# Rounding and subtracting the factors of seven-product block pairs two at a time

## The chip, the cores and the metric

The kernel runs on one core of one Trainium2 chip. The metric is the device time of one execution in microseconds (us). Lower is better. TensorE does the matmuls, VectorE (DVE in the rows) and ScalarE (ACT) work on whole 128-partition tiles, GpSimd is POOL, and SyncE (SP) issues most of the DMAs. PEld is TensorE's weight load, which runs beside its matmuls.

## The reference, cut to what matters

One layer of a decoder trunk for 512 prompt tokens and 8 sample tokens, 520 columns in all, model width 1024:

```python
z = rmsnorm(x, g1) @ w_in                         # q, k, v, o, gates, u, vb, ga, gb
y_a = (sigmoid(o) * mlstm(q, k, v, ...)) @ w_a
y_b = spatial_gate(gelu(u), rmsnorm(gelu(vb), g_v)) @ w_b
x = x + (sigmoid(ga) * y_a + sigmoid(gb) * y_b) @ w_o
up = rmsnorm(x, g2) @ w_up                        # width 2 * 2816
a, gval = split(causal_conv3(up) + c_b)
x = x + (silu(a) * gval) @ w_down
y = rmsnorm(x, g_final)
```

All of it is float32. The matmuls keep close to float32's precision by splitting each operand in two: a rounded part (hi, in the type fp32r) and the rest (lo = value - hi). A product is then hi·hi + hi·lo + lo·hi, three matmuls.

## The kernel before

**Tiling.** Data lie feature-major: 128 features on the partitions, 8 such blocks (`KT`), 520 tokens in two halves of 260 columns (`HALF`). A weight slot is 128 x 1024: eight 128 x 128 blocks side by side. Slots come in turn into two buffers `raw[0]` and `raw[1]` by SP's queue. ScalarE rounds a slot into `whi[t]` (`split`, L583, through the helper `A`, L580-581, so that every ScalarE row of the trace has L581), VectorE subtracts it into `wlo[t]` (`low`, L1079), and TensorE multiplies (`tile`, L1963; every matmul row has L1961). Two parities t alternate, so one slot is prepared while the other is multiplied.

**Block pairs.** In two places two output slots are computed together by a seven-product scheme in place of eight block products. Two neighbouring slots give a matrix of 2 x 2 blocks: a11 and a12 are the halves (512 columns, `HW`) of `raw[t0]`, a21 and a22 those of `raw[t1]`. The seven left factors are a11, a12, four sums of the blocks (`wsum`, or `dsum` in the down projection) and a22, in the order of `self.factor` (L288, L306). VectorE makes the four sums (`weight_sums` L1493, `down_weight_sums` L1705). Each factor f is rounded by ScalarE (`factor_hi`, L850, counted on the semaphore `s_ch`) and subtracted by VectorE (`factor_low`, L1488, counted on `s_pl`) into its place, half a buffer: factors 0 and 1 fill `whi[t0]` and `wlo[t0]`, factors 2 and 3 fill `whi[t1]` and `wlo[t1]`, factors 4 and 5 use t0 again and 6 uses t1. The right factors are quarters of the activations or combinations of them.

**Who waits for what.** TensorE multiplies a factor in `product` (L2175): it waits until `s_pl` has counted this factor, then issues 12 matmuls of 260 columns (4 blocks times 3 of hi and lo). The seven products of a pair follow each other, and full slots stand between pairs. ScalarE rounds factors 0 and 1 when the slot that last used t0 is done, and factors 2 and 3 when the slot that last used t1 is done (which is the last slot ahead of product 0) and the sums are there. In the down projection it waits for three of the four sums. VectorE's order in a pair is written out by hand: low of factors 0 and 1, the four sums, work on the last results, low of factors 2 and 3, and so on (`ay_pair` L1543, `down_pair` L1716).

**Where.** There are five gate pairs (q = 0 to 4, `gate_pair` L2195) and three down pairs (`down_pair` L2293 for TensorE). Product 0 of gate pair 0 begins near 354.7 us of the profiled span, those of gate pairs 1 to 4 near 376.5, 398.1, 419.6 and 441.2 us, and those of the down pairs near 782.3, 812.8 and 842.9 us. Between the first of a pair's slots and product 0 VectorE finishes the results of the pair ahead: `first_branch` (L1449, one operation) ahead of pairs 0 and 1, `branch_gated` (L1476, two operations) ahead of pairs 2 to 4. SP's queue reloads `raw[t0]` when the four sums are made (L533, L555) and `raw[t1]` when factor 6 is subtracted (L535, L559).

Of the kernel before, what the change touches and what calls it, by code (L numbers as in the profile page):

```python
# [17 lines left out]
F32 = mybir.dt.float32  # L18
F32R = mybir.dt.float32r
ALU = mybir.AluOpType  # L20
# [66 lines left out]
def hybrid_layer(nc, ins, outs):  # L87
    with ExitStack() as ctx:  # L88
# [59 lines left out]
        dsum = at("dsum", [P, 4, HW], F0 + 6688)  # L148
# [31 lines left out]
        wsum = at("wsum", [P, 4, HW], Q0 + 2 * XB)  # L180
# [5 lines left out]
        whi = [at(f"whi{t}", [P, KT * P], R0 + 8192 + (4096 + 32) * t, F32R) for t in range(2)]  # L186
        wlo = [at(f"wlo{t}", [P, KT * P], R0 + 16384 + 96 + (4096 + 64) * t, F32R) for t in range(2)]
# [87 lines left out]
        class Pair:  # L275


            def __init__(self, q):
                self.q = q
                self.n = [At(S_BY + 2 * WHOLE + 4 * q + t) for t in range(4)]  # L280
                self.of_b = q == 0
                self.t0, self.t1 = self.n[0].c % 2, self.n[1].c % 2
                self.j = WHOLE if self.of_b else 2 * q - 2
                self.a, self.d = (out_ps[self.t0][:, r, 0:HALF] for r in range(2))
                self.b, self.c = (out_ps[self.t1][:, r, 0:HALF] for r in range(2))
                r0, r1 = raw[self.t0], raw[self.t1]
                self.a11, self.a12, self.a21, self.a22 = r0[:, 0:HW], r0[:, HW:], r1[:, 0:HW], r1[:, HW:]
                self.factor = (self.a11, self.a12, wsum[:, 3, :], wsum[:, 1, :], wsum[:, 0, :], wsum[:, 2, :], self.a22)  # L288

            def place(self, w, f):  # L290

# [2 lines left out]
        class DownPair(Pair):  # L294


            def __init__(self, i):
                self.q = GATE_PAIRS + i
                self.i, self.j = i, 2 * i
                self.n = [At(S_DN + 6 * i + t) for t in range(8)]  # L300
                self.t0, self.t1 = self.n[4].c % 2, self.n[5].c % 2
                self.p1, self.p6 = (trp[t][:, :, :].rearrange("p a b -> p (a b)")[:, 0:HALF] for t in range(2))
                self.p5, self.p7 = (aux[:, t, 0:HALF] for t in range(2))
                r0, r1 = raw[self.t0], raw[self.t1]
                self.a11, self.a12, self.a21, self.a22 = r0[:, 0:HW], r0[:, HW:], r1[:, 0:HW], r1[:, HW:]
                self.factor = (self.a11, self.a12, dsum[:, 3, :], dsum[:, 1, :], dsum[:, 0, :], dsum[:, 2, :], self.a22)  # L306
                self.next_width = down_width(0 if i == DOWN_PAIRS - 1 else 1)

        def down_width(g):
# [269 lines left out]
        def _(act):  # L579
# [270 lines left out]
            def factor_hi(pr, f):  # L850

                A(pr.place(whi, f), pr.factor[f]).then_inc(s_ch, 1)

            def first_factors_hi(pr):

                act.wait_ge(w_loaded[pr.t0], pr.n[0].half(1) * 16)
                act.wait_ge(done, pr.n[0]())
                factor_hi(pr, 0)
                factor_hi(pr, 1)

            def next_factors_hi(pr):

                act.wait_ge(done, pr.n[1]())
                act.wait_ge(s_sw, 4 * pr.q + 4)
                factor_hi(pr, 2)
                factor_hi(pr, 3)

            def by_plain(i):
                n = At(S_BY + 2 * i)
# [119 lines left out]
            def down_pair(pr):  # L989
                q, n = pr.q, pr.n  # L990
                act.wait_ge(w_loaded[pr.t0], n[4].half(1) * 16)
                act.wait_ge(done, n[4]())
                factor_hi(pr, 0)
                factor_hi(pr, 1)
                act.wait_ge(s_sw, 4 * q + 3)
                act.wait_ge(done, n[5]())
                factor_hi(pr, 2)
                factor_hi(pr, 3)
                act.wait_ge(s_pd, 6 * q + 1)
                factor_hi(pr, 4)  # L1000
                A(dtmp[:, 1, :], pr.p1).then_inc(s_dc, 1)
                act.wait_ge(s_pd, 6 * q + 2)
                act.wait_ge(s_sw, 4 * q + 4)
                factor_hi(pr, 5)
                act.wait_ge(s_pd, 6 * q + 3)
                act.wait_ge(w_loaded[pr.t1], n[5].half(1) * 16)
                factor_hi(pr, 6)
                act.wait_ge(w_loaded[pr.t0], n[6].half(1) * 16)
                act.wait_ge(s_pd, 6 * q + 5)
                A(whi[pr.t0][:, 0:HW], raw[pr.t0][:, 0:HW]).then_inc(s_nh, 1)  # L1010
                act.wait_ge(s_pd, 6 * q + 6)
                A(whi[pr.t0][:, HW:pr.next_width], raw[pr.t0][:, HW:pr.next_width]).then_inc(w_hi, 3)
                split(n[7], down_width(1 if pr is pairs_d[-1] else 2))
# [62 lines left out]
        def _(dve):  # L1076
# [411 lines left out]
            def factor_low(pr, f):  # L1488

                dve.wait_ge(s_ch, 7 * pr.q + f + 1)  # L1490
                TT(pr.place(wlo, f), pr.factor[f], pr.place(whi, f).bitcast(F32), ALU.subtract).then_inc(s_pl, 1)  # L1491

            def weight_sums(pr):  # L1493

                for n in pr.n[0:2]:
                    dve.wait_ge(w_loaded[n.c % 2], n.half(1) * 16)
                TT(wsum[:, 0, :], pr.a21, pr.a22, ALU.add).then_inc(s_sw, 1)
                dve.drain()
                TT(wsum[:, 1, :], wsum[:, 0, :], pr.a11, ALU.subtract).then_inc(s_sw, 1)
                TT(wsum[:, 2, :], pr.a11, pr.a21, ALU.subtract).then_inc(s_sw, 1)  # L1500
                dve.drain()
                TT(wsum[:, 3, :], pr.a12, wsum[:, 1, :], ALU.subtract).then_inc(s_sw, 1)

            def first_gate_sum(pr):

# [4 lines left out]
            def by_plain(i):  # L1510
                n = At(S_BY + 1 + 2 * i)
                last = i == WHOLE - 1
                if i == NC:
                    unit_gated(NC * NH - 1)
                    low(n)
                    first_branch(n.plus(-2), i - 1, (i - 1) % 2)
                    x_difference(0, 1, 0)
                    unit_low(NC * NH - 1)
                    x_sum(2, KT // 2, 1)
                    dve.drain()  # L1520
                    x_difference(1, 2, 1)
                    x_difference(2, 2, 0)
                    low(n.plus(1))
                    x_combination_low(0, 1)
                    x_sum(3, KT // 2, 0)
                    dve.drain()
                    x_difference(3, 3, 2)
                    x_combination_low(2, 2)
                if last:
                    x_combination_low(1, 3)  # L1530
                    factor_low(pairs_w[0], 0)
                    factor_low(pairs_w[0], 1)
                    weight_sums(pairs_w[0])
                first_branch(n, i, i % 2)
                if last:
                    factor_low(pairs_w[0], 2)
                    factor_low(pairs_w[0], 3)
                    x_combination_low(3, 4)
                    first_gate_sum(pairs_w[0])
                else:  # L1540
                    low(n.plus(2))

            def ay_pair(pr):  # L1543
# [28 lines left out]
                if last:  # L1572
                    low(At(S_WO))
                    merged_low(pr.j)
                else:
                    factor_low(pairs_w[q + 1], 0)
                    factor_low(pairs_w[q + 1], 1)
                    weight_sums(pairs_w[q + 1])
                    if not pr.of_b:
                        merged_low(pr.j)  # L1580
# [4 lines left out]
                if last:  # L1585
                    low(At(S_WO + 1))
                else:
                    factor_low(pairs_w[q + 1], 2)
                    factor_low(pairs_w[q + 1], 3)
                    first_gate_sum(pairs_w[q + 1])  # L1590
                if not pr.of_b:
                    merged_low(pr.j + 1)
# [112 lines left out]
            def down_weight_sums(pr):  # L1705

                for n in pr.n[4:6]:
                    dve.wait_ge(w_loaded[n.c % 2], n.half(1) * 16)
                TT(dsum[:, 0, :], pr.a21, pr.a22, ALU.add).then_inc(s_sw, 1)
                dve.drain()  # L1710
                TT(dsum[:, 1, :], dsum[:, 0, :], pr.a11, ALU.subtract).then_inc(s_sw, 1)
                dve.drain()
                TT(dsum[:, 3, :], pr.a12, dsum[:, 1, :], ALU.subtract).then_inc(s_sw, 1)
                TT(dsum[:, 2, :], pr.a11, pr.a21, ALU.subtract).then_inc(s_sw, 1)

            def down_pair(pr):  # L1716
                q, n, j = pr.q, pr.n, pr.j
                part = lambda t, h: x1[:, j + t, h * HALF:(h + 1) * HALF]
                factor_low(pr, 0)
                factor_low(pr, 1)  # L1720
                down_weight_sums(pr)
                factor_low(pr, 2)
                factor_low(pr, 3)
                factor_low(pr, 4)
                factor_low(pr, 5)
                dve.wait_ge(s_pd, 6 * q + 3)
# [722 lines left out]
```

## Time and profile before

| | |
|---|---|
| median of 3 runs | 895.37 us (895.3 to 896.08) |
| the profiled execution | 896.04 us |
| its span, first to last instruction | 894.2 us |
| instructions | 18963 |
| matmuls | 7306 |
| mean TensorE clock granted | 0.996 of full speed |
| DMA | 100.44 MB, mean 112 GB/s |

How to read the rows: in a row of the timeline the columns are the start in the span, the duration (of all "x" instructions of the row, from the first's start to the last's end), the engine, the line, the operation, what it writes and reads, the shape, the count, and in brackets the idle time of the engine just before and what ended it. A duration covers the whole of an instruction, and the next one on the engine may start a little before it ends, so starts can be nearer to each other than durations. Matmuls overlap strongly: their rows last 0.28 us each, but they start 0.12 us apart.

### The profile page before, as it was taken

How to read it: one execution, taken by the hardware profiler on the slowest of the kernel's cores; microseconds unless marked ns; L12 is line 12 of the kernel's file. 1: busy time of each engine (PE TensorE's matmuls, PEld its weight loads, DVE VectorE, ACT ScalarE, POOL GpSimd, SP SyncE). 2: the span in 40 equal slices, each digit the busy share in tenths (PEclk: the TensorE clock that was granted, in tenths of full speed). 3: DMA queues.
4: the chain of work that ended last, by engine and by line, in shares of the span. 5: the costliest groups of instructions: out<-in, count | busy, mean ns of one | idle time of the engine just before them, and what ended most of it. 6: DMA issues, size and time to landing. Idle time of an engine off the chain costs nothing.

```text
span 894.2 us, 18963 instructions
## 1 busy us (share of the span) xinstructions
PE 886.6 (99%) x7306; PEld 881.9 (99%) x7306; DVE 609.9 (68%) x980; ACT 390.5 (44%) x629; POOL 133.0 (15%) x182
## 2 busy tenths in 40 slices
PE   9999999999999999999999999999999999999997
PEld 9999999999999999999999999999999999999997
DVE  7886775443885568677755777777777778966543
ACT  7545434544873334344432344444444444432333
POOL 0673000002542110000005800000000000000001
PEclk9999999999999999999999999999999999999998
DMA  6332252234872222322255222222222222333232
GB/s 214 107 131 89 77 196 101 84 100 149 291 269 69 67 76 75 116 95 95 96 197 135 89 81 94 94 94 94 94 93 86 83 91 87 99 107 93 85 106 96
DMA packets 31499, 100.44 MB, mean 112 GB/s; under 512 B 4668, under 2 KB 7260, under 8 KB 31192
## 3 DMA queue, kind: packets, MB, share of 16 engines
q1 hardware_dynamic: 29256, 92.96, 31.1%
q0 software_dynamic: 1472, 5.72, 2.1%
q10 hardware_dynamic: 720, 1.04, 0.4%
q8 instruction: 36, 0.59, 0.3%
q14 instruction: 15, 0.12, 0.0%
HBM read 92.37 MB, written 7.35 MB: 112 GB/s over the span
## 4 chain that ended last, share of the span: by engine, by line
PE 91%; POOLq 3%; issue 3%; DMA 1%; POOL 1%; ACT 0%; SPq 0%; ACTq 0%
PE out L1961 84%; PE trp L1961 3%; PE aux L1961 2%; POOLq L1939 2%; POOLq L1937 1%; PE trp L1995 1%; DMA cwb<-in_conv_wb 1%; DMA raw_pair<-in_w_slots 1%; PE aux L2153 0%; POOL y L1952 0%; POOL out_conv_old L1923 0%; ACT xg L581 0%; POOL sct L1927 0%; POOLq L1930 0%; POOLq L88 0%
## 5 line engine op out<-in xcount | busy, mean ns | idle before, releaser
L581 ACT ACTIVATE whi<-raw_pair 128x1024 fp32r<-128x1024 f32 (+4 forms) x168 | 154.2, 924 | 207.4 <-PE out L1961 195.6
L1083 DVE TENSOR_TENSOR wlo<-raw_pair,whi 128x1024 fp32r<-128x1024 f32 (+1 forms) x121 | 155.2, 1282 | 86.8 <-ACT whi L581 86.4
L1961 PE MATMUL out<-xh,whi 128*128 128x260 f32 x668 | 143.5, 289 | 0.0
L1961 PE MATMUL out<-x2h,whi 128*128 128x260 f32 x704 | 141.8, 283 | 0.0
L1961 PE MATMUL out<-x2l,whi 128*128 128x260 f32 x704 | 141.3, 282 | 0.0
L1961 PE MATMUL out<-x2h,wlo 128*128 128x260 f32 x704 | 141.2, 282 | 0.0
L1961 PE MATMUL out<-xl,whi 128*128 128x260 f32 x668 | 139.0, 282 | 0.0
L1961 PE MATMUL out<-xh,wlo 128*128 128x260 f32 x668 | 139.0, 282 | 0.0
L1961 PEld LDWEIGHTS out<-x2h,whi 128*128 128x128 f32 x704 | 108.4, 188 | 0.1
L1961 PEld LDWEIGHTS out<-x2h,wlo 128*128 128x128 f32 x704 | 108.3, 188 | 0.0
L1961 PEld LDWEIGHTS out<-x2l,whi 128*128 128x128 f32 x704 | 108.3, 188 | 0.0
L1961 PEld LDWEIGHTS out<-xh,whi 128*128 128x128 f32 x668 | 105.2, 188 | 0.7 <-issue 0.2
L1961 PEld LDWEIGHTS out<-xl,whi 128*128 128x128 f32 x668 | 104.9, 188 | 0.0
L1961 PEld LDWEIGHTS out<-xh,wlo 128*128 128x128 f32 x668 | 104.9, 188 | 0.0
L1961 PE MATMUL out<-acth,whi 128*128 128x260 f32 (+2 forms) x266 | 58.2, 284 | 0.0
L1961 PE MATMUL out<-actl,whi 128*128 128x260 f32 (+2 forms) x266 | 57.8, 282 | 0.0
L1961 PE MATMUL out<-acth,wlo 128*128 128x260 f32 (+2 forms) x266 | 57.8, 282 | 0.0
L1645 DVE TENSOR_TENSOR up<-out,rbc 128x520 f32<-128x520 f32 x44 | 30.8, 700 | 37.5 <-PE out L1961 37.3
L1945 POOL COPY nconv<-up 128x10 f32 x44 | 10.4, 237 | 240.1 <-DVEq L1646 240.1
L581 ACT ACTIVATE acth<-silu 128x520 f32 (+1 forms) x22 | 14.1, 639 | 69.8 <-DVE silu L1660 69.8
L1961 PEld LDWEIGHTS out<-acth,whi 128*128 128x128 f32 x266 | 42.9, 188 | 0.2 <-DVE wlo L1491 0.2
L1961 PEld LDWEIGHTS out<-actl,whi 128*128 128x128 f32 x266 | 42.8, 188 | 0.0
(362 smaller groups left out, 1758.0 us busy)
## 6 DMA issues: line engine op xcount, KB each, us to landing
raw_pair<-in_w_slots SPq DMA_DIRECT2D x123, 512.0 KB, 3.3
raw_pair<-in_w_dn SPq DMA_DIRECT2D x16, 448.0 KB, 3.3
c_ring<-in_C_state SPq DMA_DIRECT2D x8, 512.0 KB, 5.1
row<-scratch SPq DMA_DIRECT2D x8, 512.0 KB, 5.9
out_C_sample<-c_ring SPq DMA_DIRECT2D x8, 512.0 KB, 4.3
raw_pair<-in_w_dn SPq DMA_DIRECT2D x8, 512.0 KB, 3.5
xres<-in_x_all POOLq DMA_DIRECT2D x1, 1560.0 KB, 6.8
x<-in_x_all SPq DMA_DIRECT2D x5, 260.0 KB, 6.7
```

The lines of the kernel that those rows point to most:

```text
L581: return act.activation(out, in_, func, **kw_)
L1083: TT(wlo[p][:, 0:width], raw[p][:, 0:width], whi[p][:, 0:width].bitcast(F32), ALU.subtract)\
L1645: TT(both(up[t][:, 2:2 + TOK]), out2(n), both(rbc2[:, :]), ALU.mult).then_inc(evac[n.c % 2], 1)
L1937: pool.drain()
L1939: pool.drain()
L1945: pool.tensor_copy(nconv[:, i * 2 + t, :], up[t][:, SEQ:2 + TOK]).then_inc(s_nc, 1)
L1961: return pe.matmul(*a, **k)
L1995: m = pe.transpose(trp[b.c % 2][:, c, :], ftmp[b.c % 2][:, c * P:(c + 1) * P], ident[:, :])
```

## The change

Factors 0 and 1 lie side by side in `raw[t0]`, and their places lie side by side in `whi[t0]` and `wlo[t0]`. The four sums are put in another order in `wsum` and `dsum`, so that factors 2 and 3 lie side by side as well. Then one operation of 1024 columns rounds factors 0 and 1, another factors 2 and 3, and the same holds for the subtraction. Each raises its semaphore by 2 when it ends. The subtraction waits until both factors are rounded. TensorE's code, the order of the steps on each engine, the factors 4 to 6 and the DMAs are not edited.

```diff
@@ class Pair (and the same in DownPair, with dsum)
-                self.factor = (self.a11, self.a12, wsum[:, 3, :], wsum[:, 1, :], wsum[:, 0, :], wsum[:, 2, :], self.a22)
+                self.factor = (self.a11, self.a12, wsum[:, 0, :], wsum[:, 1, :], wsum[:, 2, :], wsum[:, 3, :], self.a22)
+                self.two = (r0, wsum[:, 0:2, :].rearrange("p a b -> p (a b)"))
@@ ScalarE
+            def two_factors_hi(pr, h):
+
+                A(whi[pr.t1 if h else pr.t0][:, :], pr.two[h]).then_inc(s_ch, 2)
+
             def first_factors_hi(pr):
...
                 act.wait_ge(done, pr.n[0]())
-                factor_hi(pr, 0)
-                factor_hi(pr, 1)
+                two_factors_hi(pr, 0)
 
             def next_factors_hi(pr):
 
                 act.wait_ge(done, pr.n[1]())
                 act.wait_ge(s_sw, 4 * pr.q + 4)
-                factor_hi(pr, 2)
-                factor_hi(pr, 3)
+                two_factors_hi(pr, 1)
@@ ScalarE, down_pair
-                factor_hi(pr, 0)
-                factor_hi(pr, 1)
+                two_factors_hi(pr, 0)
                 act.wait_ge(s_sw, 4 * q + 3)
                 act.wait_ge(done, n[5]())
-                factor_hi(pr, 2)
-                factor_hi(pr, 3)
+                two_factors_hi(pr, 1)
@@ VectorE
+            def two_factors_low(pr, h):
+
+                t = pr.t1 if h else pr.t0
+                dve.wait_ge(s_ch, 7 * pr.q + 2 * h + 2)
+                TT(wlo[t][:, :], pr.two[h], whi[t][:, :].bitcast(F32), ALU.subtract).then_inc(s_pl, 2)
+
             def weight_sums(pr):
...
-                TT(wsum[:, 0, :], pr.a21, pr.a22, ALU.add).then_inc(s_sw, 1)
-                dve.drain()
-                TT(wsum[:, 1, :], wsum[:, 0, :], pr.a11, ALU.subtract).then_inc(s_sw, 1)
-                TT(wsum[:, 2, :], pr.a11, pr.a21, ALU.subtract).then_inc(s_sw, 1)
-                dve.drain()
-                TT(wsum[:, 3, :], pr.a12, wsum[:, 1, :], ALU.subtract).then_inc(s_sw, 1)
+                TT(wsum[:, 2, :], pr.a21, pr.a22, ALU.add).then_inc(s_sw, 1)
+                dve.drain()
+                TT(wsum[:, 1, :], wsum[:, 2, :], pr.a11, ALU.subtract).then_inc(s_sw, 1)
+                TT(wsum[:, 3, :], pr.a11, pr.a21, ALU.subtract).then_inc(s_sw, 1)
+                dve.drain()
+                TT(wsum[:, 0, :], pr.a12, wsum[:, 1, :], ALU.subtract).then_inc(s_sw, 1)
```

In `down_weight_sums` the places change in the same way and the order in time stays. In the five places of VectorE's program where `factor_low(pr, 0)` and `factor_low(pr, 1)`, or 2 and 3, were called one after the other, `two_factors_low(pr, 0)` or `two_factors_low(pr, 1)` is called (in `by_plain`, `ay_pair` and `down_pair`).

## Rows read from the trace of the kernel before

**Rows 1.** The page, part 1: busy time, share of the span, instructions, by engine

```profile
PE 886.6 (99%) x7306; PEld 881.9 (99%) x7306; DVE 609.9 (68%) x980; ACT 390.5 (44%) x629; POOL 133.0 (15%) x182
```

**Rows 2.** Windows: length, busy by engine (count), granted clock, DMA share, GB/s

```profile
core 0: us, PE busy (x) PEld busy (x) DVE busy (x) ACT busy (x) POOL busy (x), PEclk, DMA share, GB/s
4.00:6.30 2.30, 1.83 (x9) 1.54 (x8) 0.83 (x2) 0.93 (x3) 0.00 (x0) 1.00 0.90 267
340.00:376.00 36.00, 36.00 (x299) 35.66 (x298) 28.43 (x40) 13.45 (x21) 0.00 (x0) 1.00 0.26 89
884.00:894.00 10.00, 4.44 (x30) 3.99 (x28) 3.18 (x10) 1.42 (x4) 1.93 (x3) 0.68 0.63 213
```

**Rows 3.** Waits of the weight load: waiter, releaser, us in total, times, longest

```profile
PEld out L1961 <- issue: 0.9, 2, 0.8
PEld out L1961 <- DVE wlo L1491: 0.2, 1, 0.2
```

**Rows 4.** Groups of instructions by form: shapes, count, busy us, mean ns, idle before

```profile
L1083 DVE TENSOR_TENSOR wlo<-raw_pair,whi 128x1024 fp32r<-128x1024 f32 x108 | 141.0, 1305 | 69.9 <-ACT whi L581 69.6
L1491 DVE TENSOR_TENSOR wlo<-wsum,whi 128x512 fp32r<-128x512 f32 x20 | 12.9, 685 | 0.2 <-ACT whi L581 0.2
L581 ACT ACTIVATE whi<-raw_pair 128x1024 fp32r<-128x1024 f32 x108 | 114.4, 1059 | 121.9 <-PE out L1961 120.8
L581 ACT ACTIVATE whi<-wsum 128x512 fp32r<-128x512 f32 x20 | 11.6, 623 | 20.2 <-PE out L1961 15.6 <-DVE wsum L1502 4.6
```

**Rows 5.** Timelines of ScalarE, VectorE and the weight load at gate pair 0

```profile
356.25 1.15 ACT L581 ACTIVATE whi<-wsum 128x512 fp32r<-128x512 f32 x2 [4.63 <-DVE wsum L1502]
...
356.91 1.29 DVE L1491 TENSOR_TENSOR wlo<-wsum,whi 128x512 fp32r<-128x512 f32 x2 [0.15 <-ACT whi L581]
...
357.36 0.19 PEld L1961 LDWEIGHTS out<-xh,wlo 128*128 128x128 f32 x1
357.72 0.19 PEld L1961 LDWEIGHTS out<-xh,whi 128*128 128x128 f32 x1 [0.17 <-issue]
```

**Rows 6.** The same timelines at gate pair 1

```profile
376.70 1.15 ACT L581 ACTIVATE whi<-wsum 128x512 fp32r<-128x512 f32 x2 [4.53 <-PE out L1961]
...
377.36 1.29 DVE L1491 TENSOR_TENSOR wlo<-wsum,whi 128x512 fp32r<-128x512 f32 x2
...
379.27 0.19 PEld L1961 LDWEIGHTS out<-xh,whi 128*128 128x128 f32 x1
```

**Rows 7.** The same timelines at gate pair 2, and VectorE's ahead of it

```profile
393.98 1.29 DVE L1491 TENSOR_TENSOR wlo<-raw_pair,whi 128x512 fp32r<-128x512 f32 x2
395.19 0.69 DVE L1497 TENSOR_TENSOR wsum<-raw_pair 128x512 f32<-128x512 f32 x1
...
398.25 1.16 ACT L581 ACTIVATE whi<-wsum 128x512 fp32r<-128x512 f32 x2 [3.51 <-PE out L1961]
...
399.36 0.70 DVE L1481 TENSOR_TENSOR merged<-merged,ftmp 128x520 f32<-128x520 f32 x1
399.97 0.69 DVE L1491 TENSOR_TENSOR wlo<-wsum,whi 128x512 fp32r<-128x512 f32 x1
...
400.83 0.19 PEld L1961 LDWEIGHTS out<-xh,whi 128*128 128x128 f32 x1
```

**Rows 8.** VectorE's timeline after gate pair 4: a subtraction 1024 wide

```profile
458.64 1.22 DVE L1083 TENSOR_TENSOR wlo<-raw_pair,whi 128x1024 fp32r<-128x1024 f32 x1
459.78 0.70 DVE L1486 TENSOR_TENSOR ml<-merged,mh 128x520 fp32r<-128x520 f32 x1
```

**Rows 9.** Timelines of VectorE, ScalarE and the weight load at down pair 0

```profile
780.53 1.22 DVE L1491 TENSOR_TENSOR wlo<-raw_pair,whi 128x512 fp32r<-128x512 f32 x2
...
783.96 1.67 ACT L581 ACTIVATE whi<-dsum 128x512 fp32r<-128x512 f32 x3 [5.21 <-DVE dsum L1713]
...
784.62 0.69 DVE L1491 TENSOR_TENSOR wlo<-dsum,whi 128x512 fp32r<-128x512 f32 x1
...
782.22 0.19 PEld L1961 LDWEIGHTS trp<-acth,whi 128*128 128x128 f32 x1
...
785.37 0.19 PEld L1961 LDWEIGHTS out<-acth,whi 128*128 128x128 f32 x1 [0.19 <-DVE wlo L1491]
```

**Rows 10.** Timelines of ScalarE and the weight load at down pair 1

```profile
813.03 1.15 ACT L581 ACTIVATE whi<-dsum 128x512 fp32r<-128x512 f32 x2 [3.86 <-PE out L1961]
...
815.43 0.19 PEld L1961 LDWEIGHTS out<-acth,wlo 128*128 128x128 f32 x1
815.55 0.19 PEld L1961 LDWEIGHTS out<-acth,whi 128*128 128x128 f32 x1
```

More of the change, by code:

```diff
@@ L305, in __init__ @@
                 self.a11, self.a12, self.a21, self.a22 = r0[:, 0:HW], r0[:, HW:], r1[:, 0:HW], r1[:, HW:]
-                self.factor = (self.a11, self.a12, dsum[:, 3, :], dsum[:, 1, :], dsum[:, 0, :], dsum[:, 2, :], self.a22)
+                self.factor = (self.a11, self.a12, dsum[:, 0, :], dsum[:, 1, :], dsum[:, 2, :], dsum[:, 3, :], self.a22)
+                self.two = (r0, dsum[:, 0:2, :].rearrange("p a b -> p (a b)"))
                 self.next_width = down_width(0 if i == DOWN_PAIRS - 1 else 1)
@@ L1530, in by_plain @@
                     x_combination_low(1, 3)
-                    factor_low(pairs_w[0], 0)
-                    factor_low(pairs_w[0], 1)
+                    two_factors_low(pairs_w[0], 0)
                     weight_sums(pairs_w[0])
@@ L1535, in by_plain @@
                 if last:
-                    factor_low(pairs_w[0], 2)
-                    factor_low(pairs_w[0], 3)
+                    two_factors_low(pairs_w[0], 1)
                     x_combination_low(3, 4)
@@ L1575, in ay_pair @@
                 else:
-                    factor_low(pairs_w[q + 1], 0)
-                    factor_low(pairs_w[q + 1], 1)
+                    two_factors_low(pairs_w[q + 1], 0)
                     weight_sums(pairs_w[q + 1])
@@ L1587, in ay_pair @@
                 else:
-                    factor_low(pairs_w[q + 1], 2)
-                    factor_low(pairs_w[q + 1], 3)
+                    two_factors_low(pairs_w[q + 1], 1)
                     first_gate_sum(pairs_w[q + 1])
@@ L1708, in down_weight_sums @@
                     dve.wait_ge(w_loaded[n.c % 2], n.half(1) * 16)
-                TT(dsum[:, 0, :], pr.a21, pr.a22, ALU.add).then_inc(s_sw, 1)
+                TT(dsum[:, 2, :], pr.a21, pr.a22, ALU.add).then_inc(s_sw, 1)
                 dve.drain()
-                TT(dsum[:, 1, :], dsum[:, 0, :], pr.a11, ALU.subtract).then_inc(s_sw, 1)
+                TT(dsum[:, 1, :], dsum[:, 2, :], pr.a11, ALU.subtract).then_inc(s_sw, 1)
                 dve.drain()
-                TT(dsum[:, 3, :], pr.a12, dsum[:, 1, :], ALU.subtract).then_inc(s_sw, 1)
-                TT(dsum[:, 2, :], pr.a11, pr.a21, ALU.subtract).then_inc(s_sw, 1)
+                TT(dsum[:, 0, :], pr.a12, dsum[:, 1, :], ALU.subtract).then_inc(s_sw, 1)
+                TT(dsum[:, 3, :], pr.a11, pr.a21, ALU.subtract).then_inc(s_sw, 1)
             def down_pair(pr):
@@ L1718, in down_pair @@
                 part = lambda t, h: x1[:, j + t, h * HALF:(h + 1) * HALF]
-                factor_low(pr, 0)
-                factor_low(pr, 1)
+                two_factors_low(pr, 0)
                 down_weight_sums(pr)
-                factor_low(pr, 2)
-                factor_low(pr, 3)
+                two_factors_low(pr, 1)
                 factor_low(pr, 4)
```

## The prediction

> **What bounds the kernel now.** I began with the page's busy shares: TensorE is busy for 99% of the span, VectorE for 68%, ScalarE for 44% [rows 1]. The windows show the same in the stretch of the first gate pair: 36.00 of 36.00 us, at the full granted clock of 2.4 GHz [rows 2]. So the end moves only with TensorE's own work, which is not edited, or with a wait put in front of it. The waits of its weight load (the first part of the engine that sees a missing factor) are small: one of 0.2 us is for the subtraction of factors, and another 0.17 us in gate pair 0 is put down to "issue" but lies at the same join [rows 3, 5]. What decides is therefore not how much work VectorE and ScalarE have in all, but how late each factor is, and I read the timelines at each join next, then the groups by form for the durations.
>
> **The durations.** A 512-wide rounding takes 0.62 us, one of 1024 takes 1.06; a 512-wide subtraction 0.685 [rows 4]. For a 1024-wide subtraction the group's mean is 1.305 us over the whole kernel [rows 4], but 1.22 in the stretch of the pairs, where the next one starts 1.14 us after it [rows 8]; two 512-wide ones take 1.21 from start to next start [rows 7]. So each fusion saves VectorE 0.07 us. For ScalarE two overlapped roundings last 1.15 us against 1.06, 0.09 saved [rows 4, 5]. Against that the first factor of the two comes later: rounding 1.06 - 0.62 = 0.44, subtraction 1.22 - 0.68 = 0.54, together 0.98 us. TensorE needs the first factor first, so this is the time at stake. Product 0 or 2 now waits for the pair; product 1 or 3 for no more than before, less some hundredths.
>
> **Factors 0 and 1.** They are prepared one slot ahead. At gate pair 2 their subtractions start at 393.98, while factors 2 and 3 of the same pair, after the four sums, are wanted only at 400.83 [rows 7], and product 0's own weights two products of 12 x 0.12 = 1.44 us earlier, about 397.95. The narrowest place is down pair 0: both subtractions there end at 780.53 + 1.22 = 781.75 and product 0 loads at 782.22 [rows 9], so even a factor 0 that comes with factor 1 is 0.47 us early. Cost 0 at all eight pairs; with a delay at the group's mean duration still 0. The sums start up to 0.37 us later where the subtraction waits for the wider rounding (pairs 1 and down pairs 1 and 2), in idle time of VectorE. In down pair 0 it does not wait, since the rounding ends long before 780.53, and the sums there, which release ScalarE at 783.96, stay where they are or come 0.07 earlier.
>
> **Factors 2 and 3, gate pair 0.** ScalarE is released by the last sum at 356.25. Before: the first rounding ends at 356.87, the subtraction begins at 356.91 and ends at 357.59, and the weights are loaded at 357.72, where the steady step of 0.12 from 357.36 would have given 357.48 [rows 5]: a stall of 0.24 already. After: rounding to 357.31, subtraction from 357.35 to 358.57, load at 358.70. Added: 0.98 us.
>
> **Gate pair 1.** ScalarE starts at 376.70, so rounding ends at 377.76; VectorE is free at 377.36, and subtracts from 377.80 to 379.02. With 0.06 (down pair 0, 785.31 to 785.37) to 0.13 us (gate pair 0) from the subtraction's end to the load this is 379.08 to 379.15, and product 2 wants 379.27 [rows 5, 6, 9]. Added: 0, with 0.1 us left of cover.
>
> **Gate pairs 2 to 4.** Here two operations for the results of the pair ahead stand before the subtraction in VectorE's queue, so it starts at 399.97 though the rounding (398.25 + 1.06 = 399.31) has ended. The 0.07 saved earlier in this queue brings it to 399.90. It ends at 401.12 and the load follows at 401.18 to 401.25, against 400.83 [rows 7]. Before, the end at 400.66 met it just in time. Added: 0.35 to 0.42, I take 0.39, and the same in pairs 3 and 4, where the distance from ScalarE's release to the subtraction is again 1.72 us: 1.17 us in three pairs. If VectorE is a little earlier than I think it stays some 0.3 each; at a duration of 1.305 it is 0.47.
>
> **Down pair 0.** VectorE works without a break here and the sum releases ScalarE at 783.96. Before: the first subtraction begins at 784.62, ends at 785.31, and the load comes at 785.37 after 0.19 us idle [rows 9]. After: 0.98 later, 786.35. Added: 0.98, or 0.91 if the 0.07 saved ahead reaches the sums.
>
> **Down pairs 1 and 2.** Release at 813.03, rounding to 814.09, subtraction from 814.13 to 815.35, load at 815.41 to 815.48; wanted at 815.55 [rows 10]. Added: 0, with about 0.1 us left; at worst 0.1 each.
>
> What else waits: factor 4's rounding is queued behind the wide one on ScalarE, which ends 0.09 earlier than the two; its subtraction likewise comes earlier. The reload of `raw[t0]` follows the sums and has several us until it is used; that of `raw[t1]` follows factor 6. Nothing else in the change has a cost. The increments of 2 are new for these semaphores only in size, and I price them at 0, between -0.1 and +0.1 at each of the two unhidden joins.
>
> **The sum.** 0.98 + 0 + 1.17 + 0.98 + 0 = 3.13 us. A delay of TensorE goes to the end in full: behind the gates it is busy throughout, and its later releasers are themselves started by its results. The profiled execution took 896.04 us, 1.84 more than its span of 894.2; with the change it would be 899.2. It lies at the upper edge of the three runs (895.3 to 896.08), so from the median 895.37 the forecast is 898.5 us.
>
> The page "VectorE: DVE Perf Modes" of the Trainium skill, section "The TRN2 errata — SBUF-src ops pay a fixed extra latency per instruction", says that the fixed cost lies between instructions, so that one large tile pays it once, and it advises wide tiles; by its formula for a float32 tensor_tensor, (N + 151) / 0.96 ns, I estimate 1.224 us for 1024 columns. The trace agrees with 1.22. That rule speaks for the change and knows nothing of who waits for the first half; what it would bring alone is the second rival.
>
> **The rivals.**
> *Only two joins show.* If VectorE's queue ahead of gate pairs 2 to 4 is earlier by 0.4 us after the change than my 0.07 (the merged results wait for TensorE and ScalarE too, and may close up), pairs 2 to 4 stay hidden: + 1.96, so 897.3 us. For it: the cover before was just enough in three pairs, with no idle time of the load there. Against it: VectorE runs from 393.98 on without a gap down to the subtraction, and only 0.07 is taken out of that.
>
> *The saved fixed costs reach the end; not slower.* The mechanism: VectorE, not TensorE, paces the pairs, above all the unbroken stretch ahead of down pair 0, so 16 fused subtractions at 0.07 give 1.1 us: 894.3 us. It decides from the point at which rounding and subtraction of both factors end no later than the first factor did, 1.31 us after the release; the rows make it 2.28. Against it also: TensorE's waits for VectorE at these joins are under 0.5 us in all, so no more than that can be had unless TensorE waits longer than the rows show. By the skill's page alone, fewer instructions are always a gain, and this is its case.
>
> *The clock falls.* The gaps ahead of product 2 grow from 0.24 to 1.2 us in two places. In the last 10 us of the span, where TensorE is busy for 4.44, the granted clock averages 0.68, so part of it is at the lower level of 1.2 GHz; but between 4.00 and 6.30, with 0.47 us idle, it is 1.00 [rows 2]. Each of the seven products takes 1.44 us; if three of them after each of the two gaps ran at half clock, 2 x 3 x 1.44 = 8.6 us are added to 3.1: 907 us. The page "TensorE: Matmul & The Clock Gate", Part 1, has the same two levels and idleness as what brings the lower one; no row here shows a fall after a gap as short as 1.2 us.
>
> *It does not do what it says*: the semaphore would be raised before the whole width is written, or TensorE would not feel the wait: 895.4 us.
>
> **How the numbers follow.** A measurement of this kernel can tell 0.2%, 1.8 us, from no change. Forecast (two large and three small stalls, 897.9 to 899.3): 0.68. Only two joins: 0.16. Saved costs reach the end: 0.06. The clock: 0.04. No effect: 0.06. The slower side of the bound is at 897.2: the forecast gives 0.66 of its 0.68, the first rival 0.11 of 0.16 (its 897.3 is at the edge), the clock 0.04, together 0.81. Same: 0.02 + 0.05 + 0.06 from no effect + 0.02 of the saved costs = 0.15. Faster: 0.04. The range reaches down to 896.9, which takes in most of the first rival and medians that are off by some tenths, and up to 900.0, with 0.47 in each of gate pairs 2 to 4, 0.1 in gate pair 1 and the two down pairs, and some tenths of the runs' own spread; the clock, the saved costs and no effect are left out.
>
> **What would show it.** The weight load should have five waits for the fused subtraction: at gate pair 0 and down pair 0 about 1.1 to 1.2 us, at gate pairs 2 to 4 about 0.3 us (0.39 less the 0.07 by which durations overlap the step), and none at gate pair 1 and down pairs 1 and 2. The 1024-wide subtractions should take 1.22 us, and the matmul count and clock should not change. I am wrong if pair 2's product 2 loads on the 0.12 us step, if the stalls are there and the span has not grown by their sum (then something later gave it back), or if product 0 waits anywhere.

## The result and the profile after

Over eight runs each, the changed kernel takes 898.72 us (898.28 to 899.44) and the kernel before 895.66 us (895.08 to 896.8). The ratio is 1.0033, with a 95% interval of 1.0023 to 1.0043: slower by about 3 us (2.1 to 3.9). The profiled execution takes 898.83 us with a span of 897.0. All ratios, here and below, are of fast runs alone: one slow execution of eleven in split_two_big (4973.73 us) and one of twelve in early (2245.13 us) are not in them.

The page of the changed kernel says what the totals did: its length and its busy shares.

```profile
span 897.0 us, 18947 instructions
...
PE 885.9 (99%) x7306; PEld 880.8 (98%) x7306; DVE 609.3 (68%) x964; ACT 388.9 (43%) x613; POOL 133.2 (15%) x182
```

Against [rows 1] VectorE and ScalarE have 16 instructions fewer each, VectorE 0.6 us and ScalarE 1.6 us less to do, TensorE the same 7306 matmuls; and the span is 2.8 us longer. The waits of the weight load in the changed kernel (to be read against [rows 3]; L1499 is the wide subtraction):

```profile
PEld out L1963 <- issue: 3.5, 5, 1.3
PEld out L1963 <- DVE wlo L1499: 1.2, 1, 1.2
```

The waits of its matmuls name the wide subtraction at all five places:

```profile
PE out L1963 <- DVE wlo L1499: 2.6, 5, 1.1
```

The kernel before had two waits on "issue"; now there are five. One of them (1.14 us at 6.4 us in the span) belongs to the start of the kernel. The other four are the joins of factor 2 at gate pairs 0 and 2 to 4; the wait of 1.2 us is down pair 0. The weight load's timeline has these four loads, each the first of a product 2, and between the first two of them the load of product 2 at gate pair 1 (380.35) with the one ahead of it, which keeps its step of 0.12 us:

```profile
358.80 0.19 PEld L1963 LDWEIGHTS out<-xh,whi 128*128 128x128 f32 x1 [1.30 <-issue]
...
380.23 0.19 PEld L1963 LDWEIGHTS out<-xh,wlo 128*128 128x128 f32 x1
380.35 0.19 PEld L1963 LDWEIGHTS out<-xh,whi 128*128 128x128 f32 x1
...
402.31 0.19 PEld L1963 LDWEIGHTS out<-xh,whi 128*128 128x128 f32 x1 [0.34 <-issue]
...
424.27 0.19 PEld L1963 LDWEIGHTS out<-xh,whi 128*128 128x128 f32 x1 [0.34 <-issue]
...
446.22 0.19 PEld L1963 LDWEIGHTS out<-xh,whi 128*128 128x128 f32 x1 [0.34 <-issue]
```

A load lasts 0.19 us and the next starts 0.12 us after it starts, so an idle time of 0.34 is a delay of 0.34 + 0.07 = 0.41 us. Below, "delay" is always this: the distance between two starts less 0.12. A single one is good to about 0.01 us.

The chain at gate pair 0 after the change, ScalarE then VectorE, to be read against [rows 5]; then at gate pair 2, against [rows 7]; then at down pair 0 with its load, against [rows 9]:

```profile
356.30 1.06 ACT L583 ACTIVATE whi<-wsum 128x1024 fp32r<-128x1024 f32 x1 [4.81 <-DVE wsum L1510]
357.46 1.23 DVE L1499 TENSOR_TENSOR wlo<-wsum,whi 128x1024 fp32r<-128x1024 f32 x1 [0.68 <-ACT whi L583]
...
399.38 1.06 ACT L583 ACTIVATE whi<-wsum 128x1024 fp32r<-128x1024 f32 x1 [3.56 <-PE out L1963]
400.98 1.22 DVE L1499 TENSOR_TENSOR wlo<-wsum,whi 128x1024 fp32r<-128x1024 f32 x1
...
786.23 1.58 ACT L583 ACTIVATE whi<-dsum 128x1024 fp32r<-128x1024 f32 x2 [5.27 <-DVE dsum L1717]
787.39 1.22 DVE L1499 TENSOR_TENSOR wlo<-dsum,whi 128x1024 fp32r<-128x1024 f32 x1 [0.64 <-ACT whi L583]
788.67 0.19 PEld L1963 LDWEIGHTS out<-acth,whi 128*128 128x128 f32 x1 [1.20 <-DVE wlo L1499]
```

At gate pair 0 ScalarE starts at 356.30, nearly as before (356.25), but the first weights that TensorE can use are complete at 357.46 + 1.23 = 358.69 instead of 357.59.

The accounts: delays of 1.37 (gate pair 0), 3 x 0.41 (gate pairs 2 to 4) and 1.27 (down pair 0) make 3.87 us, against 0.24 and 0.26, 0.50 in all, before: 3.37 us more. The last group of sums at the end starts 3.28 us later (889.69 against 886.41), so the stalls arrive there in full, to a tenth. The span is only 2.8 longer because of the tail, which the last section explains.

### The profile page after: what moved, and what is told of

It is laid out like the page before. It is cut to its first block, busy times and chain, and to the rows that moved or that the text cites. A ratio compares the mean times of both kernels' runs of the same rounds, so it can differ in the third digit from the quotient of the medians.

```text
span 897.0 us, 18947 instructions
## 1 busy us (share of the span) xinstructions
PE 885.9 (99%) x7306; PEld 880.8 (98%) x7306; DVE 609.3 (68%) x964; ACT 388.9 (43%) x613; POOL 133.2 (15%) x182
## 3 DMA queue, kind: packets, MB, share of 16 engines
q10 hardware_dynamic: 720, 1.04, 0.4%
## 4 chain that ended last, share of the span: by engine, by line
PE 83%; DVE 5%; issue 4%; POOLq 3%; DMA 2%; DVEq 2%; POOL 1%; ACT 1%; SPq 0%; ACTq 0%
PE out L1963 76%; PE trp L1963 3%; PE aux L1963 2%; POOLq L1941 2%; POOLq L1939 1%; DMA raw_pair<-in_w_slots 1%; PE trp L1997 1%; DMA cwb<-in_conv_wb 1%; DVE wlo L1499 1%; DVE wlo L1085 1%; DVEq L1506 0%; DVE dtl L1707 0%; ACT whi L583 0%; PE aux L2155 0%; DVE wsum L1510 0%
```

## The experiments

The theory: product 2 waits for the first half of its factors, which comes about 1 us later as half of a wide operation; all the loss is there. The rivals were: a share from factors 0 and 1 or from the new places of the sums; the fixed costs saved reaching the end; for the smaller stalls, another cause than VectorE's queue.

The median of before moves between the series of runs (895.6 to 895.9 us), so the ratio is what is compared. The delays are those of one profiled execution each, and a sum of them is good to some hundredths.

| kernel | delay, gate pair 0 | gate pairs 2 to 4, each | down pair 0 | all | median | ratio to before |
|---|---|---|---|---|---|---|
| before | 0.24 | 0 | 0.26 | 0.50 | 895.66 | |
| changed | 1.37 | 0.41 | 1.27 | 3.87 | 898.72 | 1.0033 (1.0023 to 1.0043) |
| only01 | 0.71 | 0 | 0.18 | 0.89 | 895.68 | 0.9999 (0.999 to 1.0008) |
| only23 | 1.74 | 0.48 | 1.34 | 4.52 | 899.18 | 1.0037 (1.0024 to 1.0051) |
| split_two_big | 0.16 | 0.41 | 0.19 | 1.57 | 896.65 | 1.0008 (0.9998 to 1.0017) |
| hidden_only | 0.14 | 0 | 0.19 | 0.33 | 895.48 | 0.9995 (0.9986 to 1.0004) |
| round_only | 0.38 | 0 | 0.66 | 1.04 | 896.25 | 1.0012 (1.0003 to 1.002) |
| subtract_only | 1.13 | 0.40 to 0.46 | 1.31 | 3.71 | 898.84 | 1.0035 (1.0022 to 1.0048) |
| between | 1.07 | 0.51 (product 4) | 1.27 | 3.87 | 899.17 | 1.0044 (1.0031 to 1.0057) |
| early | 0 | 0.51 (product 4) | 0 | 1.53 | 896.71 | 1.0009 (1.0 to 1.0018) |
| between_later | 1.01 | 0 | 1.27 | 2.28 | 897.64 | 1.0021 (1.0012 to 1.003) |
| best_split | 0 | 0 | 0 | 0 | 895.28 | 0.9992 (0.9983 to 1.0001) |
| best_wide | 0 | 0 | 0 | 0 | 894.96 | 0.9992 (0.9983 to 1.0001) |

**Which pair of factors.** Both helpers choose by `h` (0: factors 0 and 1; 1: factors 2 and 3):

```diff
+                if h == 0:          # only01; h == 1 in only23
                     A(whi[pr.t1 if h else pr.t0][:, :], pr.two[h]).then_inc(s_ch, 2)
+                else:
+                    factor_hi(pr, 2 * h)
+                    factor_hi(pr, 2 * h + 1)
... (the same for the subtraction)
```

> Only factors 0 and 1 are rounded and subtracted as one; 2 and 3 go one by one, with the sums in the new places. Theory (the first of factors 2 and 3 comes 0.98 us later, and product 2 waits): no stall of product 0 anywhere, the stalls of the kernel before stay at 0.17 and 0.19 us of load idle, time as before, 895.7 us, within 0.3. Rival A (part of the loss comes from the fusion of 0 and 1, through later sums or a later reload): 0.5 to 1.5 us over before, and idle of the weight load at product 0 or later sums at pairs 1 to 4. Rival B (the new places of the sums cost): every join a little later, over 896.5 us.

> Only factors 2 and 3 are rounded and subtracted as one, in all eight pairs. Theory: all of the loss is here: 3.1 us over before, 898.8 us, with load idle of 1.3 us at gate pair 0, 1.2 at down pair 0 and, since 0.07 us of VectorE's queue is no longer saved ahead of them, 0.41 in place of 0.34 at gate pairs 2 to 4 (so up to 0.2 more than the changed kernel). Rival A: 0.5 to 1.5 us less than the changed kernel.

Only01 measures as before (0.9999), with no stall at a product 0; its sums have the new places too, so the places cost nothing that can be told. Only23 has all of the loss: 1.0037. One expectation was wrong: in only01 the delay at gate pair 0 was 0.71 us and not 0.24, though the pair there is split. These are its first sum, its rounding and its load:

```profile
353.81 0.69 DVE L1513 TENSOR_TENSOR wsum<-raw_pair 128x512 f32<-128x512 f32 x1 [2.36 <-DMA raw_pair<-in_w_slots]
...
356.77 1.15 ACT L583 ACTIVATE whi<-wsum 128x512 fp32r<-128x512 f32 x2 [5.19 <-DVE wsum L1518]
...
358.25 0.19 PEld L1971 LDWEIGHTS out<-xh,whi 128*128 128x128 f32 x1 [0.65 <-issue]
```

The sums wait for a transfer. Counted from the load that opens the slot ahead (348.88 in before, 348.92 here), the first sum starts at 4.41 us in before and at 4.89 here, and between 4.13 and 4.89 over these profiles; it moves with the transfer and not with the edit (4.89 also in only23, where factors 0 and 1 are split). From ScalarE's start to the load the distance is then the same in all runs of a kind: 1.47 or 1.48 us where both are split (before 357.72 - 356.25, only01 358.25 - 356.77), 2.50 or 2.51 where both are fused (changed, only23, between). So the fusion's own price from ScalarE's start on is 1.03 us at gate pair 0, and the later sums add 0.1 us in the changed kernel's profile. At down pair 0 the same distance is 1.41 where both are split (785.37 - 783.96) and 2.44 where both are fused (788.67 - 786.23): again 1.03.

**The two places and the hidden ones.** The condition is `not (h == 1 and pr.q in (0, 5))` in split_two_big and `h == 0 or pr.q in (1, 6, 7)` in hidden_only (down pairs have q = 5 to 7).

> The changed kernel, but factors 2 and 3 of gate pair 0 and of down pair 0 go one by one. Theory: the two large stalls go back to 0.17 and 0.19 us of load idle, the three of 0.34 at gate pairs 2 to 4 stay: 1.2 us over before, 896.9 us, 1.9 under the changed kernel. Rival (the delays are given back later, or one stall hides another): less than 1.2 us under the changed kernel, and new idle of the load behind the two places.

> Factors 0 and 1 fused in all pairs, factors 2 and 3 only in gate pair 1 and down pairs 1 and 2, where some tenth of a us of cover was left. Theory: as before, 895.7 us within 0.3, with 11 operations fewer on each of VectorE and ScalarE and no new load idle: an operation saved there is worth nothing. Rival (the saved fixed costs reach the end): 0.07 us for each fused subtraction, 0.8 us under before, 894.9 us.

Both came as the theory has them: removing two stalls left the other three at 0.41. In hidden_only 11 fused operations on each engine move no time that can be told (0.9995, interval over 1), and the delays alone, 0.33 against 0.50, would give 0.9998. That fits no gain beyond the stalls, but the interval doesn't exclude the rival's 0.8 us.

**The two halves of the price.** In round_only the rounding is always fused and the subtraction for `h == 0` alone; subtract_only is the reverse.

> The changed kernel, but factors 2 and 3 are subtracted one by one; their rounding stays one operation. Theory: the first factor loses only the 0.44 us of the wider rounding, and only where VectorE waits for ScalarE: +0.45 to 0.5 at gate pair 0 and at down pair 0 (load idle about 0.65 each), 0 at gate pairs 2 to 4, where the rounding ends 0.6 us before VectorE is free. 0.9 us over before, 896.6 us. Rival (stall is the subtraction's alone): as before, 895.7. Rival (any wide operation costs the same): 1.5 us over before.

> The changed kernel, but factors 2 and 3 are rounded one by one; their subtraction stays one operation, so it waits for the second rounding. Theory: the two roundings take 1.15 us against 1.06, so the first factor comes 0.09 us later than in the changed kernel at gate pair 0 and down pair 0, and no later at gate pairs 2 to 4: 3.25 us over before, 898.9 us; gate pair 1 and down pairs 1 and 2 keep about 0 of cover and may show up to 0.1 each. Rival (the loss is shared between the two operations by their widths): about half of the changed kernel's loss, 897.2.

Down pair 0 in round_only, ScalarE, VectorE and the load:

```profile
783.92 1.58 ACT L583 ACTIVATE whi<-dsum 128x1024 fp32r<-128x1024 f32 x2 [5.26 <-DVE dsum L1725]
...
785.02 2.50 DVE L1497 TENSOR_TENSOR wlo<-dsum,whi 128x512 fp32r<-128x512 f32 x4 [0.58 <-ACT whi L583]
...
785.76 0.19 PEld L1971 LDWEIGHTS out<-acth,whi 128*128 128x128 f32 x1 [0.59 <-DVE wlo L1497]
```

The rounding alone costs 0.48 us there (0.66 against the 0.18 of only01), and at gate pair 0 the distance from ScalarE's start is 1.90 against 1.47. The delay there is only 0.38 us, less than expected, because this profile has the earliest sums (4.13 us after the load that opens the slot ahead). Gate pairs 2 to 4 do not feel the wider rounding. With the subtraction fused and the rounding split the distance is 2.59, the 0.09 us more of two roundings; at gate pair 1 and down pairs 1 and 2, where up to 0.1 us was expected, subtract_only has 0.02 each. The ratio of round_only, 1.0012, is 0.5 us more than its delays say; its interval holds them.

**VectorE's queue.** In between, the wide subtraction stands ahead of the second operation for the last results:

```diff
                 TT(both(ftmp[g][:, :]), both(ftmp[g][:, :]), out2(n), ALU.mult).then_inc(evac[n.c % 2], 1)
+                if ahead is not None:     # two_factors_low(pairs_w[q + 1], 1)
+                    ahead()
                 dve.drain()
                 TT(merged[:, j, :], merged[:, j, :], ftmp[g][:, :], ALU.add).then_inc(s_ms, 1)
```

> The changed kernel with one step moved in VectorE's queue ahead of gate pairs 2 to 4: the wide subtraction stands between the two operations for the last results (after the one that empties the accumulator, ahead of the addition into merged). Theory: it starts when the rounding ends, 0.5 us earlier, so the load of product 2 comes on the step again at gate pairs 2 to 4: 1.2 us under the changed kernel, 897.5 us, with the idle of 1.3 and 1.2 us unchanged. Rival (the stalls there are TensorE's handoff and not VectorE's queue): as the changed kernel, 898.7. Rival (the later addition delays the merged results): new idle of the load at the first output-projection slots, over 898 us.

The time did not fall: 899.17 us, where 897.5 was expected. The stall at product 2 was gone, as the theory has it, but a new one of 0.51 us stood at product 4. ScalarE, VectorE and the load:

```profile
402.30 0.64 ACT L583 ACTIVATE mh<-merged 128x520 fp32r<-128x520 f32 x1 [2.15 <-DVE merged L1489]
402.84 0.37 ACT L583 ACTIVATE gtmp<-out 128x260 f32<-128x260 f32 x1
...
403.24 0.42 DVE L1526 TENSOR_TENSOR ftmp<-gtmp,out 128x260 f32<-128x260 f32 x1 [0.98 <-ACT gtmp L583]
...
405.00 0.19 PEld L1974 LDWEIGHTS out<-th,whi 128*128 128x128 f32 x1 [0.44 <-issue]
```

The addition into `merged` came later, ScalarE stood at the rounding of these results for 2.15 us, and behind it in its queue stood the copy of product 0 (`gtmp`), for which VectorE waited 0.98 us ahead of factor 4's subtraction. The third rival had the later addition and the time right, and the place wrong: the stall is inside the pair and not at the output projection. In between_later these two steps stand behind factor 4 of the next pair:

```diff
                 A(gtmp[:, 0, :], pr.a).then_inc(s_pc, 1)
                 factor_hi(pr, 4)
+                if q >= 2:
+                    merged_hi(pairs_w[q - 1].j + 1)
... (the same for merged_low behind factor_low(pr, 4) on VectorE; the old calls stay for the last pair alone)
```

> As the run in which the wide subtraction stands between VectorE's two operations for the last results, and in addition the rounding and the subtraction of these results (merged_hi and merged_low of the pair's second slot) stand behind factor 4 of the next pair, on both engines. Theory (in the run before the stall moved from product 2 to product 4, because the late addition held back ScalarE's copy of product 0, which stands behind merged_hi in its queue): no load idle at gate pairs 2 to 4 at all, delays only at gate pair 0 (0.9 to 1.7 us, by when the transfer for the sums lands) and down pair 0 (1.27): 1.2 to 1.5 us under the changed kernel, 897.4 us. Rival (product 4 is late for the wide subtraction itself, which takes VectorE too long): the 0.44 us of load idle at product 4 stay, 898.7.

No delay is left at gate pairs 2 to 4, and the ratio falls from 1.0044 to 1.0021. So the stalls of the changed kernel there were VectorE's queue, and the one of between came from the work on the last results standing ahead of factor 4.

**Versions meant to beat both.** Early adds two edits to between and splits factors 2 and 3 in gate pair 0 and down pair 0; best_wide adds the same to between_later, and best_split to hidden_only:

```diff
                 TT(wsum[:, 1, :], wsum[:, 2, :], pr.a11, ALU.subtract).then_inc(s_sw, 1)
-                TT(wsum[:, 3, :], pr.a11, pr.a21, ALU.subtract).then_inc(s_sw, 1)
                 dve.drain()
                 TT(wsum[:, 0, :], pr.a12, wsum[:, 1, :], ALU.subtract).then_inc(s_sw, 1)
+                TT(wsum[:, 3, :], pr.a11, pr.a21, ALU.subtract).then_inc(s_sw, 1)
...
-                act.wait_ge(s_sw, 4 * pr.q + 4)
+                act.wait_ge(s_sw, 4 * pr.q + 3)
... (ahead of factor_hi(pr, 5))
+                act.wait_ge(s_sw, 4 * q + 4)
...
-            dve.memset(acc[:, :], 0.0).then_inc(s_accf, 1)
             down_pair(pairs_d[0])
+            dve.memset(acc[:, :], 0.0).then_inc(s_accf, 1)
```

> The version that should beat both: factors 2 and 3 fused except in gate pair 0 and down pair 0; the wide subtraction between the two operations as in the run before; in the gate pairs the sum for factor 2 is made third and ScalarE waits for three sums; the clearing of the norm accumulator, 0.49 us on VectorE ahead of down pair 0, comes after that pair. Theory: no stall at any of the eight pairs, also not the 0.24 us and 0.26 us of the kernel before: 0.5 us under before, 895.2 us, near what the runs can tell; the trace has the verdict. Rival (the old stalls have another cause than VectorE's late sums): the load idle of 0.17 and 0.19 us stays, and 895.7 us.

> Factors 2 and 3 fused only in gate pair 1 and down pairs 1 and 2, nothing moved in the work on the last results; the sum for factor 2 made third in the gate pairs with ScalarE waiting for three sums, and the clearing of the norm accumulator put behind down pair 0. Theory: no load idle at any pair: 0.5 us of local delay fewer than before, 895.2 us, with the run's own uncertainty as large. Rival (the earlier rounding does not help, since VectorE does the subtraction at the same time): 0.17 and 0.19 us of load idle stay, 895.7.

> As the run above, but factors 2 and 3 fused in gate pairs 2 to 4 too, with the order of the first run of this call there. Theory: no load idle at any pair either, and the same time, 895.2 us: fewer operations on VectorE and ScalarE are worth nothing while TensorE waits for none. Rival (saved operations are a gain in themselves): under the run above by 0.2 us or more.

Early missed its 895.2 us: it measured 896.71, because it carries the stall of between, 0.51 us in each of three pairs. In the two others there is none: these are all waits of the weight load in best_wide from 340 to 870 us, and neither is at a block pair.

```profile
PEld aux L1979 <- POOLq L1957: 0.3, 1, 0.3
PEld out L1979 <- DVE wlo L1092: 0.2, 1, 0.2
```

Both kernels have a ratio of 0.9992, with an interval that just holds 1: the 0.5 us that the trace shows gone (0.9994) fits, and is not shown by the times. The wide form and the split form cannot be told apart: their ratios are the same, and their medians differ by 0.32 us (894.96 against 895.28), less than the half microsecond that the tail alone can make (last section). So the rival of best_wide, that saved operations are worth 0.2 us or more, is not excluded.

**The wait in front of an operation that raises its semaphore by 2.** Two handoffs from ScalarE to VectorE in the changed kernel, first of a full slot, then of factors 2 and 3 at gate pair 1; both roundings and both subtractions are 1024 wide:

```profile
366.37 1.06 ACT L583 ACTIVATE whi<-raw_pair 128x1024 fp32r<-128x1024 f32 x1 [0.80 <-PE out L1963]
367.46 1.22 DVE L1085 TENSOR_TENSOR wlo<-raw_pair,whi 128x1024 fp32r<-128x1024 f32 x1 [0.72 <-ACT whi L583]
...
377.83 1.06 ACT L583 ACTIVATE whi<-wsum 128x1024 fp32r<-128x1024 f32 x1 [4.65 <-PE out L1963]
378.99 1.23 DVE L1499 TENSOR_TENSOR wlo<-wsum,whi 128x1024 fp32r<-128x1024 f32 x1 [0.52 <-ACT whi L583]
```

The full slot's subtraction, which raises its semaphore by 1, starts 0.03 us after the rounding ends (367.43), the other 0.10 us (378.89). The trace shows the difference: a subtraction that raises by 1 holds its wait in itself, while none of the 48 operations of ScalarE and VectorE in the changed kernel that raise by 2 or 3 does; their wait is an instruction of its own. This is L1498, `wait_ge` in `two_factors_low` (duration in ns: shortest, median, longest; the kernel before has no such instruction for `factor_low`):

```profile
L1498 DVEq EVENT_SEMAPHORE  x16: 21/21/21, 350.1 to 847.6; - x16
```

That it goes with the operation's own raise, and not with the width or with the rounding's raise, three other rows say: a subtraction 384 wide that raises by 3 (L1740 of the kernel before, 821.68 + 0.53 to 822.31) also starts 0.10 us after its rounding; in subtract_only, where the roundings raise by 1, the wide subtraction still starts 0.10 us after them; in round_only a 512-wide one, which raises by 1, starts 0.04 us after a wide rounding that raises by 2 (784.98 to 785.02). ScalarE has the same thing: at down pair 0 its wide rounding starts 0.09 us after the sum ends (785.45 + 0.69 to 786.23), the 512-wide one in the kernel before 0.04 (783.23 + 0.69 to 783.96). There too it is not the width: full-slot roundings, 1024 wide, start 0.02 us after TensorE has counted its slot as done, the fused ones of gate pairs 1 to 4 start 0.07 us after it. No run kept the wide operations and raised by 1. As an estimate from these rows, that would give back 0.12 us at down pair 0 and 0.07 at gate pair 0, of the 1.0 and 1.1 us that are lost there.

## Why the prediction was right

*The sum* was 3.13 us and the ratio gives 2.96 us (0.0033 x 895.66), medians 3.06. 898.5 was forecast and 898.72 measured. The interval of the ratio is 0.9 us to either side, so the times alone cannot weigh the terms, and that the sum is met to 0.2 us is in part luck. The delays of the traces can: they add up to 3.37, 0.24 more than forecast, and the terms below share it.

*Gate pair 0, forecast 0.98.* The profile has 1.13 more. The wider rounding (0.43) and the wider subtraction (0.53) came as worked out. Mis-sized was the raise by 2, which was priced at 0, between -0.1 and +0.1: the subtraction starts 0.07 us later for it (357.36 to 357.46, where 0.04 was taken), which makes the 1.03. The last 0.1 us are the sums, which a transfer released 0.09 us later in this profile. ScalarE's release there was treated as fixed, which it is not.

*Gate pairs 2 to 4, forecast 0.39 each.* 0.41 each, for the reason given: the subtraction waits for VectorE's queue and not for ScalarE, so the wider rounding costs nothing. The wide subtraction starts 0.92 us ahead of the step on which the load is wanted (400.98 against 402.31 - 0.41 = 401.90), the narrow one 0.86 us ahead (399.97 against 400.83): 0.06 earlier, where 0.07 was forecast.

*Gate pair 1 and down pairs 1 and 2, forecast 0.* They load on the step, as shown for gate pair 1. The cover was thinner than the forecast 0.1 us, since the raise by 2 counts here too, on both engines: the subtraction starts at 378.99 and ends at 380.22, and the load comes at 380.35, 0.13 us later, where gate pair 0 needs 0.11 (358.69 to 358.80). It held by about 0.02.

*Down pair 0, forecast 0.98, or 0.91 with the 0.07 saved ahead.* 1.01 more: 1.03 from ScalarE's start to the load, 0.05 by which ScalarE starts later after the sum, less 0.08 that the fusion of factors 0 and 1 gives back (0.26 to 0.18 in only01). The parts were named, and the raise by 2 was again the term that was too small, by 0.12 on the two engines together.

*Factors 0 and 1, forecast 0.* Only01 shows it: no delay at a product 0, and a ratio of 0.9999.

*The rivals.* Only two joins: refuted, the other three stalls are in every profile that has the wide subtraction at that place of the queue (changed, only23, split_two_big, subtract_only). The saved fixed costs: refuted in sign for the change as a whole; the wide operation that pays its fixed cost once is the one that comes late. That a part of the saved cost reaches the end where no stall stands against it is not excluded (hidden_only, best_wide). That it does nothing: refuted. The clock: refuted, by the windows of the gate pairs and from down pair 0 on in the changed kernel (length, busy time of each engine, granted clock, DMA share, GB/s), where the clock is 1.00 through gaps of up to 1.3 us:

```profile
340.00:466.00 126.00, 124.40 (x1032) 123.51 (x1031) 89.72 (x132) 48.88 (x74) 1.10 (x3) 1.00 0.30 101
786.00:870.00 84.00, 83.01 (x693) 82.80 (x693) 48.73 (x75) 27.04 (x38) 0.00 (x0) 1.00 0.34 99
```

*The signs.* Five waits of the load came, where they were said to be, of 1.30 and 1.20 us (1.1 to 1.2 forecast) and three of 0.34 (about 0.3); no product 0 waits. One sign of being wrong did show: the span grew by 2.8 us and not by the 3.37 of the delays. Something later gave some 0.5 us back, the clock of the last matmuls (last section), on which the forecast had no word.

## What to carry to other kernels

Where a consumer takes two halves in turn, fuse the two producing steps only if the first half has at least as much slack as the wide operation lasts longer than the narrow one, on every engine that the consumer's chain waits for (here 0.43 + 0.53 us), plus what a raise by 2 costs in front of each (here 0.05 and 0.07 us). Read that slack at each join by itself: for factors 2 and 3 it was enough in three of eight pairs, for factors 0 and 1 in all eight. No gain from instructions saved on engines with idle time could be told here; moving a step in a queue to win half a microsecond has to be followed through every engine's queue up to the next consumer, or the stall only moves.

## What the runs showed of the hardware that I had not expected

**The tail runs at either clock, and not by the edit.** In the kernel before, the window from just ahead of the last small matmuls to the end (length, TensorE busy, granted clock, DMA share, GB/s):

```profile
887.50:894.00 6.50, 2.06 (x8) 0.51 0.67 227
```

The same window in the changed kernel:

```profile
890.80:897.00 6.20, 1.15 (x8) 0.63 0.70 237
```

The eight matmuls themselves, from TensorE's timeline of the kernel before:

```profile
887.55 1.21 PE L1961 MATMUL aux<-ident,nd 120*128 120x120 f32 x4 [0.56 <-DVE nd L1818]
888.55 1.06 PE L1961 MATMUL trp<-ident,nd 120*128 120x120 f32 x4
```

And from that of the changed kernel:

```profile
890.83 0.70 PE L1963 MATMUL aux<-ident,nd 120*128 120x120 f32 x4 [0.55 <-DVE nd L1820]
891.37 0.61 PE L1963 MATMUL trp<-ident,nd 120*128 120x120 f32 x4
```

The eight matmuls take 2.06 us in before, where the granted clock is 0.52 from 887.5 to 889.7, near the lower of the two levels (1.2 GHz), and 1.15 in the changed kernel, where it is 1.00 from 890.8 to 892.0 (2.4 GHz), each after the same short idle time (0.56 and 0.55 us idle ahead of the first four). The clock falls in both profiles, in the one as these matmuls begin, in the other after they have ended. From the last sums to the end before has 894.2 - 886.41 = 7.79 us and the changed kernel 897.0 - 889.69 = 7.31. That is the 0.48 us by which the span grew less than the stalls. It isn't the edit: hidden_only and best_split fuse the same factors, and the two rows last 0.70 and 0.61 us in the one, 1.09 and 1.06 in the other; only01 has 1.21 and 1.06, best_wide 0.70 and 0.61. With one profile of each kernel, what decides it is open. A difference of half a microsecond between two single profiles of this kernel can be this alone.

**A raise by 2 has its price.** Where an operation raises its semaphore by more than 1, its wait is an instruction of its own (21 ns long on VectorE), and the operation starts 0.07 us later behind its releaser on VectorE (0.10 against 0.03 us; all nine fused subtractions of the changed kernel that waited for their rounding have it, and 68 full-slot ones of the same width have 0.03) and 0.05 us later on ScalarE (0.07 against 0.02 us after TensorE's count of a finished slot at gate pairs 1 to 4, and 0.09 against 0.04 after the sum at down pair 0).
